# RWKV-7 sample recurrence from elementwise passes to chunked matrix products, with a feature-major output norm

## The reference

```
S = S * w_t + (S @ -kk_t) (kk_t * a_t)^T + v_t k_t^T     # per head, state 64 x 64, value by key
y_t = S @ r_t
y = (y - mean) * rsqrt(var + 64e-5) * ln_w + ln_b         # per head
y = y + sum(r * k * r_k) * v;   o_b = y * g
x = x + W_out(sigmoid(G_a) * P_a(HGRN2) + sigmoid(G_b) * P_b(o_b))
x = x + MoE_top4of32(RMSNorm(x))                          # clamped SwiGLU experts, D_FF 1024
```

## Time and profile before

| | us |
|---|---|
| runs shown | 1499.76, 1502.67, 1497.7 |
| median | 1499.76 |
| profiled execution, own time | 1504.84 |
| its span (first to last instruction) | 1502.9 |
| PE busy | 1378.4 (92%) |
| DVE busy | 431.2 (29%) |
| ACT busy | 233.5 (16%) |
| POOL busy | 221.2 (15%) |
| mean granted clock of PE | 0.948 |

### The profile page before, as it was taken

The page is one execution under the profiler, slowest core; times in us unless marked ns, Lnnn a source line. Parts: engine busy times, 40 slices in busy tenths (PEclk is TensorE's granted clock), DMA queues, the critical chain, the costliest instruction groups (busy, mean ns, idle before and its releaser), DMA issues.

```text
span 1502.9 us, 17606 instructions
## 1 busy us (share of the span) xinstructions
PE 1378.4 (92%) x6984; PEld 667.4 (44%) x6984; DVE 431.2 (29%) x908; ACT 233.5 (16%) x497; POOL 221.2 (15%) x195
## 2 busy tenths in 40 slices
PE   6999879919889999999999999999999999999997
PEld 5777547818777463333333333333333333333332
DVE  2226792592443051211211211111111112112112
ACT  2154101401220120110110110010011101100113
POOL 4001799991000400000000000000000000000000
PEclk9999779856889979999999999999999999999999
DMA  9334322101042467999999999999999999999994
GB/s 265 122 112 135 94 62 86 32 26 40 25 159 80 171 266 288 429 429 429 427 430 428 428 430 427 430 427 429 429 428 430 428 429 429 428 430 427 430 427 189
DMA packets 63196, 451.15 MB, mean 300 GB/s; under 512 B 5163, under 2 KB 33509, under 8 KB 37974
## 3 DMA queue, kind: packets, MB, share of 16 engines
q1 hardware_dynamic: 55680, 441.24, 71.2%
q0 software_dynamic: 2064, 6.77, 1.7%
q10 hardware_dynamic: 5414, 2.61, 0.6%
HBM read 445.39 MB, written 5.21 MB: 300 GB/s over the span
## 4 chain that ended last, share of the span: by engine, by line
PE 70%; DMA 17%; DVE 8%; ACT 3%; issue 2%; SPq 0%; ACTq 0%; DVEq 0%
PE bank L918 22%; DMA ring<-in_expert_w_gu_dram 17%; PE bank L946 10%; PE bank L427 9%; PE bank L880 5%; PE bank L851 3%; ACT arena L964 2%; PE bank L788 2%; PE bank L769 2%; DVE ring L1495 2%; PE bank L473 1%; DVE ring L1472 1%; PE bank L913 1%; DVE ring L1467 1%; PE bank L815 1%
## 5 line engine op out<-in xcount | busy, mean ns | idle before, releaser
L918 PE MATMUL bank<-ring,arena 128*64 128x512 f32 x2024 | 452.9, 597 | 2.2 <-DMA ring<-in_expert_w_gu_dram 2.2
L918 PEld LDWEIGHTS bank<-ring,arena 128*64 128x64 f32 x2024 | 142.4, 137 | 280.1 <-issue 246.0
L946 PE MATMUL bank<-ring,arena 128*64 128x512 f32 x1024 | 226.8, 596 | 15.7 <-ACT arena L964 15.7
L964 ACT ACTIVATE arena<-bank 128x512 f32<-128x512 f32 (+6 forms) x231 | 115.1, 529 | 566.2 <-PE bank L946 222.2
L427 PE MATMUL bank<-arena,ring 128*128 128x288 f32 (+1 forms) x608 | 161.7, 425 | 1.5 <-ACT arena L964 1.5
L1728 DVE TENSOR_SCALAR arena<-bank 128x256 f32<-128x256 f32 x64 | 24.2, 421 | 406.6 <-PE bank L918 406.6
L946 PEld LDWEIGHTS bank<-ring,arena 128*64 128x64 f32 x1024 | 70.7, 137 | 151.2 <-issue 127.9
L427 PEld LDWEIGHTS bank<-arena,ring 128*128 128x128 f32 x608 | 119.2, 199 | 41.7 <-issue 4.2
L964 ACT ACTIVATE arena<-arena 128x512 f32<-128x512 f32 (+7 forms) x73 | 56.0, 779 | 502.3 <-DVE arena L1728 493.4
L1740 DVE COPY arena<-bank 64x512 f32<-64x512 f32 x32 | 22.2, 694 | 349.6 <-PE bank L946 349.6
L851 PE MATMUL bank<-arena 128*64 128x512 f32 (+1 forms) x396 | 95.5, 599 | 0.0
(11 more groups left out here) (316 smaller groups left out, 1215.2 us busy)
## 6 DMA issues: line engine op xcount, KB each, us to landing
ring<-in_expert_w_gu_dram SPq DMA_DIRECT2D x126, 2048.0 KB, 22.3
ring<-in_expert_w_down_dram SPq DMA_DIRECT2D x64, 2048.0 KB, 18.6
ring<-in_w_in_dram SPq DMA_DIRECT2D x23, 1024.0 KB, 5.3
ring<-in_w_out_dram SPq DMA_DIRECT2D x4, 1024.0 KB, 8.6
arena<-in_expert_w_gu_dram SPq DMA_DIRECT2D x3, 1024.0 KB, 18.8
ring<-in_state_hgrn_dram POOLq DMA_DIRECT2D x1, 2048.0 KB, 11.8
out_dram<-ring ACTq DMA_DIRECT2D x1, 2048.0 KB, 8.7
ring<-in_w_branch_a_dram SPq DMA_DIRECT2D x2, 1024.0 KB, 5.5
```

The costliest lines, as they stand in the source:

```text
L918: ins = mm(bank[q % 2][64 * (q // 2):64 * (q // 2) + 64, :], gu_lhs(c), gu_cols(c, x, first)[:, q * 512:(q + 1) * 512], start=(c == 0), st ...
L946: ins = mm(bank[1][64 * h:64 * h + 64, :], dn_lhs(j, r), w_slot(GU + j)[:, r * D + h * 512:r * D + (h + 1) * 512], start=(j == 0 and r == ...
L964: return nc.scalar.activation(out, in_, f, **kw)
```

## The change

The sample recurrence becomes one chunk of 4 steps per sequence, worked out on PE for two groups of 4 heads (32 rows each, so 128 rows). The state is transposed to key-by-value (16 transposes). Scores of all sample rows are masked to pairs of the same sequence (`smp_mask`). The old state's part is 64 products of 8 columns (`u0`). The triangular solve is three steps of product and add (`smp_solve`). The new states are 16 products of 512 columns over rows spread by sequence (`vexp_s`, `uexp_s`), added to the decayed old state and transposed back (16 transposes). ACT copies PSUM out at each step, DVE masks and adds, and POOL makes `vexp_s` and the decay product of 128x2048 and adds the norm bias to the bonus.

All this stands between the last projection tile and `hgrn_prompt(0)`, with three gate tiles in it. `hgrn_sample`, `hgrn_prompt(1)` and the units keep their calls of `gate_tile`, so the 16 tiles are used up after unit 2. The trips through DRAM go. States load and store by 8 DMAs each on POOL's queue, one per sequence, in pieces of 64 floats.

The RWKV output stays feature-major. The y products have their operands exchanged (64-column weights, 128 moving columns). The head sums of the norm are products with `ones64`, two per unit into bank 3. `ob_center`, Square, Ln, Exp and `ob_final` replace `center_b`, `gate_b` and the 12 transposes. The norm of one unit's output runs in the next unit (the sample rows' in unit 0), that of unit 3 during the first branch. The bonus becomes 4 products of 288 columns with `ones64`, and g 4 products likewise. `gate_a(u - 1)` moves to the head of DVE's units 1 to 3. Two parameter rows more go over ACT's queue, two broadcasts less over POOL's. SP's wait on `ysm_st` goes.

```diff
             pe.wait_ge(S("bonus_in"), 1)
-            for t, (o, rows) in enumerate(TILES):
-                for q in range(4):
-                    i = mm(bank[6][0:rows, t * 8 + 2 * q:t * 8 + 2 * q + 2], z1[:, q * NT + o:q * NT + o + rows],
-                           head2, start=True, stop=True)
-            done(i, "bonus_done")
+            for q in range(4):
+                done(mm(bank[4 + q][:, 0:NT], ones64, z1[:, q * NT:(q + 1) * NT], start=True, stop=True), "bonus_done")
+        if n == 13:
             pe.wait_ge(S("recip"), 2)
-            for t, (o, rows) in enumerate(TILES):
-                b = bank[(4, 5, 7)[t]]
-                done(mm(b[0:rows, :], glT[:, o:o + rows], g2, start=True, stop=True), "g_done")
-            pe.wait_ge(S("smp_in"), 1)
-            srcs = [fm[0], wS, fm[1], fm[9], fm[3], fm[2]]
-            for a, src in enumerate(srcs):
-                b = bank[(4, 5, 7)[a % 3]]
-                if a < 3:
-                    pe.wait_ge(S("g_evac"), a + 1)
-                else:
-                    pe.wait_ge(S("smp_evac"), a - 2)
-                for q in range(4):
-                    v = src[:, q * NS:(q + 1) * NS] if a == 1 else src[:, q * NT + NP_:(q + 1) * NT]
-                    i = nc.tensor.transpose(b[0:NS, q * P:(q + 1) * P], v, ident)
-                done(i, "smp_T")
-    pe.wait_ge(S("smp_evac"), 6)
...
+            for q in range(4):
+                pe.wait_ge(S("bonus_evac"), q + 1)
+                done(mm(bank[4 + q][:, 0:NT], g2[:, q * P:(q + 1) * P], glT, start=True, stop=True), "g_done")
+    pe.wait_ge(S("s0_loaded"), 16 * NB)
+    for q in range(4):
+        pe.wait_ge(S("g_evac"), q + 1)
+        for b in range(4):
+            i = nc.tensor.transpose(bank[4 + q][:, b * P:(b + 1) * P], S_s[:, b * 512 + q * P:b * 512 + (q + 1) * P], ident)
+        done(i, "smp_pe")
...
+    def smp_scores():
+        pe.wait_ge(S("smp_dve"), smp_dve["ins"] + 1)
+        for G in range(2):
+            pe.wait_ge(S("smp_act"), smp_act["s0"] + G + 1)
+            for hh in range(4):
+                q, r, o, c0 = smp_head(G, hh)
+                mm(bank[4 + G][o, 0:64], Bn[r, c0:c0 + NS], AR[r, :, c0:c0 + NS], start=True, stop=True)
+                i = mm(bank[4 + G][o, 64:128], Kn[r, c0:c0 + NS], AR[r, :, c0:c0 + NS], start=True, stop=True)
+            done(i, "smp_pe")
+        for G in range(2):
+            pe.wait_ge(S("smp_act"), smp_act["s0"] + G + 3)
+            for hh in range(4):
+                q, r, o, c0 = smp_head(G, hh)
+                for a, v in enumerate((vR[r, c0:c0 + NS], bg[r, q * NS:(q + 1) * NS], kg[r, q * NS:(q + 1) * NS])):
+                    i = mm(bank[6 + G][o, a * 64:(a + 1) * 64], v, ident[r, r], start=True, stop=True)
+            done(i, "smp_pe")
+        pe.wait_ge(S("pj_evac"), E_BLOCK)
+        for G in range(2):
+            for b in range(NB):
+                for hh in range(4):
+                    q, r, o, c0 = smp_head(G, hh)
+                    c = (hh // 2) * 64 + 8 * b
+                    i = mm(bank[2 + G][r, c:c + 8], S0T[r, q * 512 + b * 64:q * 512 + (b + 1) * 64],
+                           AR[r, :, c0 + TS * b:c0 + TS * (b + 1)], start=True, stop=True)
+            done(i, "smp_pe")
+    def smp_solve():
+        for G in range(2):
+            pe.wait_ge(S("smp_dve"), smp_dve["mask"] + G + 1)
+            pe.wait_ge(S("smp_act"), smp_act["stack"] + G + 1)
+            pe.wait_ge(S("smp_act"), smp_act["u0"] + G + 1)
+            mm(bank[4 + G][:, 0:64], PMs[:, G * 512 + 256:G * 512 + 384], stk[:, G * 192:G * 192 + 64], start=True, stop=False,
+               skip_group_check=True)
+            for hh in range(4):
+                q, r, o, c0 = smp_head(G, hh)
+                c = G * 128 + (hh // 2) * NS
+                i = mm(bank[4 + G][o, 0:64], u0[r, c:c + NS], ident[r, r], start=False, stop=True, skip_group_check=True)
+            done(i, "smp_pe")
+        gate_tile()
+        for j in range(3):
+            for G in range(2):
+                if j == 0:
+                    pe.wait_ge(S("smp_act"), smp_act["rhs"] + G + 1)
+                else:
+                    pe.wait_ge(S("smp_dve"), smp_dve["z"] + 2 * (j - 1) + G + 1)
+                done(mm(bank[6 + G][:, 0:64], PMs[:, G * 512:G * 512 + P], (U_s if j else rhs_s)[:, G * 64:(G + 1) * 64],
+                        start=True, stop=True), "smp_pe")
+        for G in range(2):
+            pe.wait_ge(S("smp_dve"), smp_dve["z"] + 4 + G + 1)
+            for hh in range(4):
+                q, r, o, c0 = smp_head(G, hh)
+                out, c = bank[2 + hh // 2][r, G * NS:(G + 1) * NS], G * 512 + NS * hh
+                mm(out, U_s[o, G * 64:(G + 1) * 64], PMs[o, c + P:c + P + NS], start=(G == 0), stop=False, skip_group_check=True)
+                i = mm(out, stk[o, G * 192:G * 192 + 64], PMs[o, c + 3 * P:c + 3 * P + NS], start=False, stop=(G == 1),
+                       skip_group_check=True)
+        done(i, "smp_pe")
+    def smp_states():
+        for G in range(2):
+            pe.wait_ge(S("smp_pool"), smp_pool["vexp"] + G + 1)
+            for hh in range(4):
+                q, r, o, c0 = smp_head(G, hh)
+                i = mm(bank[4 + q][r, :], stk[o, G * 192 + 128:G * 192 + 192], vexp_s[o, G * 512:(G + 1) * 512], start=True,
+                       stop=False, skip_group_check=True)
+        for G in range(2):
+            pe.wait_ge(S("smp_dve"), smp_dve["uexp"] + G + 1)
+            for hh in range(4):
+                q, r, o, c0 = smp_head(G, hh)
+                i = mm(bank[4 + q][r, :], stk[o, G * 192 + 64:G * 192 + 128], uexp_s[o, G * 512:(G + 1) * 512], start=False,
+                       stop=True, skip_group_check=True)
+            done(i, "smp_pe")
+        gate_tile()
+        for q in range(4):
+            pe.wait_ge(S("smp_dve"), smp_dve["new"] + q + 1)
+            for b in range(4):
+                i = nc.tensor.transpose(bank[4 + q][:, b * P:(b + 1) * P], S_s[:, q * 512 + b * P:q * 512 + (b + 1) * P], ident)
+            done(i, "smp_pe")
+    smp_scores()
+    gate_tile()
+    smp_solve()
+    smp_states()
...
+            if lev == 0:
+                ob_sums(u, y_buf)
+            if lev == 2:
+                pe.wait_ge(S("ob_sq"), u + 1)
+                ob_sums(u, sq_buf)
...
+    def ob_center(idx):
+        n = 4 * NS if idx == 0 else 256
+        dve.wait_ge(S("ob_sums"), 2 * idx + 1)
+        step(v.scalar_tensor_tensor(out=y_buf[idx], in0=bank[3][:, 0:n], scalar=-1.0 / DB, in1=y_buf[idx], op0=ALU.mult,
+                                    op1=ALU.add), "ob_c")
+    def ob_final(idx):
+        q0, nq, o, n = (0, 4, NP_, NS) if idx == 0 else (2 * ((idx - 1) % 2), 2, P * ((idx - 1) // 2), P)
+        y = y_buf[idx]
+        cols = [slice((q0 + q) * NT + o, (q0 + q) * NT + o + n) for q in range(nq)]
+        dve.wait_ge(S("ob_rstd"), idx + 1)
+        step(v.tensor_tensor(y, y, sq_buf[idx], ALU.mult))
+        dve.wait_ge(S("smp_pool"), smp_pool["bias"] + 4)
+        for q in range(nq):
+            i = v.scalar_tensor_tensor(out=y[:, q * n:(q + 1) * n], in0=y[:, q * n:(q + 1) * n], scalar=pc(par, 42 + q0 + q),
+                                       in1=bv[:, cols[q]], op0=ALU.mult, op1=ALU.add)
+        step(i)
+        dve.wait_ge(S("g_evac"), 4)
+        ob3, g3 = (a.rearrange("p (q t) -> p q t", q=4)[:, q0:q0 + nq, o:o + n] for a in (obT, gF))
+        step(v.tensor_tensor(ob3, y.rearrange("p (q t) -> p q t", q=nq), g3, ALU.mult), "ob_done")
...
-    pool.wait_ge(S("smp_evac"), 6)
-    for a in range(6):
...
-    S3, T3 = (a.rearrange("p (v k) -> p v k", k=DB) for a in (S_s, tmp_s))
-    def row_sums(out):
-        w = DB // 2
-        while w >= 1:
-            o = T3[:, :, 0:w] if w > 1 else out.unsqueeze(2)
-            step(g.tensor_tensor(o, T3[:, :, 0:w], T3[:, :, w:2 * w], ALU.add))
-            w //= 2
...
-    for t in range(TS):
-        step(g.tensor_tensor(T3, S3, k_row(t, 3), ALU.mult))
-        row_sums(sa_s)
-        step(g.tensor_tensor(S3, S3, k_row(t, 1), ALU.mult))
-        step(g.tensor_tensor(T3, v_col(sa_s), k_row(t, 4), ALU.mult))
-        step(g.tensor_tensor(S3, S3, T3, ALU.subtract))
-        step(g.tensor_tensor(T3, v_col(v_s[:, t * 32:(t + 1) * 32]), k_row(t, 2), ALU.mult))
-        step(g.tensor_tensor(S3, S3, T3, ALU.add))
-        step(g.tensor_tensor(T3, S3, k_row(t, 0), ALU.mult))
-        row_sums(y_s[:, t * 32:(t + 1) * 32])
-    for x in range(2):
-        pool.dma_start(rwkv_s[0][:, :, 32 * x:32 * x + 32, :].rearrange("b h v k -> h b (v k)"),
-                       S_s[64 * x:64 * x + 64, :]).then_inc(S("rws_out"), 16)
-        pool.dma_start(ysm_dram[x].rearrange("h b t v -> (h b) (t v)"), y_s[64 * x:64 * x + 64, :]).then_inc(S("ysm_st"), 16)
-    pool.wait_ge(S("ysm_st"), 32)
+    for q in range(4):
+        pool.wait_ge(S("bonus_evac"), q + 1)
+        step(g.tensor_scalar(bv[:, q * NT:(q + 1) * NT], bv[:, q * NT:(q + 1) * NT], par[:, 46 + q:47 + q], None, ALU.add), "smp_pool")
```

(47 more changed lines are left out.)

313 lines of the change are left out of this document (161 added, 152 removed).

## The result

The changed kernel takes 1446.66 us (median of 4 runs, 1443.55 to 1449.31) against 1500.94 for the kernel before beside it (1497.7 to 1502.67). The ratio is 0.964, 95% interval 0.9612 to 0.9668. Forecast: 1475, range 1452 to 1492. The sign and the cause of the gain were right; the gain is 54 us, over twice the 24.5 of the sum.

A forecast was written before the change was run, and what follows sets the result against it. PE was taken to set the order before the first expert load, with DVE holding it up in two stretches. Terms +39 -23.5 -35.5 +2 -5.5 -1 gave -24.5, so 1499.76 became 1475 us; range 1452 to 1492.

The forecast's parts named there:

- What bounds the kernel: Before 488 us PE sets the order and DVE delays it in two stretches; the end moves one to one with attention.
- C: Rival: DVE's slow passes had another cause than POOL, so only the sample block is added: 1534 us; chance 3%.
- 1, projection: Projection stage: 9.4 us of PE work removed, 4 us added; PE's last projection ends at 150.4 instead of 155.8.
- 2, the sample block: New recurrence block on PE ahead of HGRN: 47 us, from 150.4 to 197.5, delaying HGRN's start by 39 us.
- low bound of 31: Sample block's lower bound in us: small products at 0.06, state products at 0.21, full clock.
- The drain on a change of tiling mode: Sample block changes tiling mode some ten times; a drain would come on top of 47 us, but was given no price.
- 3, HGRN: HGRN stage falls from 75.7 to 52 us, counted as -23.5, with no POOL pass left there.
- 4, units: RWKV units: unit 1 -35.5 us, the norm's PE part +2, unit 3 without gate tiles -5.5, units 0 and 2 unchanged.
- operands exchanged, no change: RWKV units' y products: 16 of 128 columns by 64 instead of 64 by 128, priced as no change.
- 5, end of attention: End of attention: 12 transposes and their evacuation go, two sums of 0.43 us come: -1 us.
- Rival A: Array keeps its clock and overlaps tiles: sample block costs 33 us, unit 3 saves 9, time 1457; chance 24%.
- Rival B: Slower than before: small products run singly at 1.2 GHz through the sample block; 1500 to 1511 us; chance 7%.

## Why the prediction was half right

- **What bounds the kernel, and C.** Right. The first expert load moved by 51.4 us and the end with it. The runs without passes and with fills show GpSimd's reading passes as the cause of both stretches. (The waits of 18.0 and 16.9 us that the prediction puts in unit 1 are sums over all four units; unit 1's own are 16.0 and 14.8.)
- **1, projection.** Forecast -5.4, measured -5.5. The start, which I left alone, came 3.5 us later, of which at most 1.4 is the two DMAs'; the rest goes with the clock.
- **2, the sample block. This is the step that failed most.** It is 15.2 of the 30.5 us by which the stages miss the forecast. The mechanism was right, the size was not: 31.8 against 47. By its terms: transposes 3.7, measured 3.7 to the next starts. Small products 12.2 (0.095 each), measured about 7.3. State products 6.9 (0.43 each), measured 3.59. Waits 2, measured 0.9. Clock 7, measured 1.7, all in the first gate tile. That is 4.9 + 3.3 + 1.1 + 5.3 = 14.6 of the 15.2. In three cases I took a row with less overlap, or at a lower clock, than the new code has. Nor did the start of a product keep its length at half clock, as the 0.095 assumed: 0.03 us a record became 0.054. The low bound of 31 is also added up wrong: its terms give 18.0, and with waits and tiles 32.2, so the block came out at the bound. Alone the block would have left the time inside the range (1475 - 15.2 = 1460). It fell outside by the terms below that stood at nothing, the output products above all (7.0).
- **The drain on a change of tiling mode**, which the prediction cites from the Trainium skill's page TensorEngine Tiling (Array Packing), Key Properties, does not show. The block changes mode some ten times, with no gap over 0.2 us in its rows but the 0.73 us that waits for ACT. (The profile models the ends of products, so a short one could be hidden in them.)
- **3, HGRN.** Forecast 52, measured 46.7. Sample updates have a period of 6.0 us with the gate tile, as worked out. The first prompt half is 8.0 instead of 9.5, at a clock of 1.00 instead of 0.52 (9.6 at 0.82 when the changed kernel is run again). The second is 15.1 instead of 17.3, and not by the clock, which is 0.90 before and 0.89 after: a wait for ACT shrank from 2.73 to 0.46. It is 0.46 in the kernel before without passes too, so this was also the passes' doing. PE in time order, before, then after:

```profile
221.18 2.98 PE L556 MATMUL bank<-arena,ring 32*128 32x128 f32 x32 [2.73 <-ACT ring L964]
...
219.23 2.92 PE L646 MATMUL bank<-arena,ring 32*128 32x128 f32 x32 [0.46 <-ACT ring L1062]
```

- **4, units.** Unit 1 fell to 43.1. The norm's own cost is too small to be told from the clock: L785 starts 33.7 us into unit 2 of after, 32.9 when the changed kernel is run again, and the same line 33.1 in the kernel before without passes. But "operands exchanged, no change" was wrong, a term put at nothing without a row: the exchange gives back 7.0 us in all. With the norm at its forecast +2, norm and output part come to about -5 over the four units (an estimate). Unit 3's missing tiles gave 6.2, forecast 5.5.
- **5, end of attention.** Forecast -1, measured -1.1. Behind it 4.0 us more, from a fall of the clock that did not come. The changed kernel itself took 1012.9 there when run again, and the kernel before without passes 1011.9, so most of this moves by itself.
- **Rival A** is what happened: block 33 forecast, 31.8 measured; unit 3 saves 9, measured 7. Its time was 1457; the output products, HGRN's halves and the part behind the first load are more than the missing 10 us, and the late start took some back. The range's low end (1452) left all of these out because each one alone stood at nothing. Of these the part behind the first load is luck.
- **Rival B** did not happen, but half its mechanism is real. With twice the small products a pause and a long stretch at half clock came, and they cost 13.5 instead of 5; but they did not run singly, 0.11 each and not 0.17.

## What to carry to other kernels

Before pricing what replaces a GpSimd pass, price what the pass does to its neighbours: here 62 us hung on an engine that the chain of waits hardly named. For small products read the tile positions of successive instructions in the new code: if rows and columns alternate, take the overlapped price (here 0.06 and 0.22 us), and not a middle. Keep the clock as a term of its own: at half clock the overlapped products still overlapped, at about twice the price (0.11 and 0.39). It moved the same block between 30.2 and 31.8 us. An exchange of operands that makes the weights 64 wide is worth its own line in the sum.

## What the runs showed of the hardware

- GpSimd fills did not slow DVE instructions with two SBUF inputs: with 152 us of them the form kept its 0.69 us. Passes that read did: about 4.5 us each in the slow pair of the earlier trace rows.
- Less work is not always shorter: with 122 products fewer the block took 32.8 us instead of 31.8, with the clock at 0.50 for 10 us of it. What lowered the clock is open.
- Neighbouring 32-row by 64-column tiles in alternation run a 512-column fp32 product in 0.22 us at full clock and 0.39 at half; three in a row on the same tile it was 0.63, at a clock of 0.51.
- A long string of small products has a pause of 1.7 to 2.0 us in which PE waits for nothing that the profile shows, at the same instruction in two kernels that are the same up to it. Its cause is open.
- The first pair of projection tiles took 4.27 us in two kernels, 5.74 to 5.95 in eight and 7.03 to 7.20 in four. It goes with the granted clock where that is on record (0.50 from 18 to 21 us for 5.94); a printed clock of 1.00 ahead of the first record of it says nothing.
